# Gated MLP of a small transformer stack: the last product of two hidden groups as seven half products of sums

## The reference

```python
f_in = _rmsnorm(h, g_pre_ffn[l])
gt = jnp.einsum("bsd,df->bsf", f_in, w_gate[l])
up = jnp.einsum("bsd,df->bsf", f_in, w_up[l])
f = jnp.einsum("bsf,fd->bsd", jax.nn.silu(gt) * up, w_down[l])
h = h + _rmsnorm(f, g_post_ffn[l])
```

## Time and profile before

| | |
|---|---|
| runs, median of 3 | 1795.46 us (1795.06 to 1796.2) |
| profiled execution, own time | 1796.07 us |
| its span in the trace | 1794.3 us |
| granted TensorE clock, mean | 0.993 |
| busy: PE, DVE, ACT | 97%, 63%, 45% |

### The profile page before, as it was taken

How to read it: one execution, slowest core, us unless ns; L and a number is a source line. 1 busy time by engine, 2 the same in 40 slices (tenths; PEclk the granted TensorE clock), 3 DMA queues, 4 the chain that set the end, 5 groups by cost and what they waited for, 6 DMA issues and landing times.

```text
span 1794.3 us, 21666 instructions
## 1 busy us (share of the span) xinstructions
PE 1746.8 (97%) x8311; PEld 1435.7 (80%) x8311; DVE 1136.0 (63%) x1988; ACT 808.1 (45%) x1543; POOL 38.1 (2%) x87
## 2 busy tenths in 40 slices
PE   8999999999999999989999999999999999999998
PEld 7887888888887777677888888788887788888886
DVE  6666358787854666865868786488977543243345
ACT  7433344444434656754444344432857532232233
POOL 0000000000001121010000000000000000000000
PEclk9999999999999999999999999999999999999999
DMA  7222443333133111115142312232100333333331
GB/s 248 80 72 85 138 117 94 106 112 89 47 98 83 60 59 60 48 47 176 58 142 71 118 51 90 71 96 92 47 12 14 102 97 106 94 94 98 102 94 59
DMA packets 195751, 158.32 MB, mean 88 GB/s; under 512 B 5248, under 2 KB 161280, under 8 KB 195648
## 3 DMA queue, kind: packets, MB, share of 16 engines
q1 hardware_dynamic: 194240, 154.16, 28.5%
q0 software_dynamic: 400, 1.25, 0.3%
q10 hardware_dynamic: 1008, 1.53, 0.2%
HBM read 154.81 MB, written 2.10 MB: 87 GB/s over the span
## 4 chain that ended last, share of the span: by engine, by line
PE 89%; DVE 6%; ACT 3%; issue 1%; DMA 0%; POOL 0%; DVEq 0%; SPq 0%; ACTq 0%
PE ps L896 29%; PE ps L898 28%; PE ps L897 28%; PE ps L1356 1%; PE ps L952 1%; ACT sb L1827 1%; PE ps L1250 0%; DVE sb L2046 0%; ACT sb L1562 0%; DVE sb L2074 0%; DVE sb L2048 0%; PE ps L1011 0%; DVE sb L2528 0%; PE ps L1221 0%; PE ps L1204 0%
## 5 line engine op out<-in xcount | busy, mean ns | idle before, releaser
L896 PE MATMUL ps<-sb,sb 128*128 128x512 f32 (+4 forms) x2499 | 958.6, 390 | 9.0 <-ACT sb L1827 5.2
L898 PE MATMUL ps<-sb,sb 128*128 128x512 f32 (+4 forms) x2499 | 938.5, 380 | 0.0
L897 PE MATMUL ps<-sb,sb 128*128 128x512 f32 (+4 forms) x2499 | 938.3, 380 | 0.0
L2048 DVE TENSOR_TENSOR sb<-sb,sb 128x512 fp32r<-128x512 f32 x604 | 390.8, 690 | 260.9 <-ACT sb L1562 258.3
L896 PEld LDWEIGHTS ps<-sb,sb 128*128 128x128 f32 (+1 forms) x2499 | 464.0, 188 | 113.9 <-issue 13.6
L1562 ACT ACTIVATE sb<-sb 128x512 fp32r<-128x512 f32 x604 | 347.1, 622 | 440.1 <-PE ps L898 438.2
L898 PEld LDWEIGHTS ps<-sb,sb 128*128 128x128 f32 (+1 forms) x2499 | 463.6, 188 | 89.2
L897 PEld LDWEIGHTS ps<-sb,sb 128*128 128x128 f32 (+1 forms) x2499 | 464.3, 189 | 83.4 <-issue 0.2
L1719 ACT ACTIVATE sb<-sb 128x512 f32<-128x512 f32 x64 | 40.3, 630 | 105.5 <-DVE sb L2321 105.5
L2330 DVE TENSOR_TENSOR sb<-sb,sb 128x1024 fp32r<-128x1024 f32 x42 | 51.4, 1224 | 39.5 <-ACT sb L1724 39.5
L2528 DVE SCALAR_TENSOR_TENSOR sb<-sb,sb,sb 128x512 f32<-128x512 f32 x90 | 67.4, 749 | 1.9
(11 more groups left out here) (216 smaller groups left out, 1082.1 us busy)
## 6 DMA issues: line engine op xcount, KB each, us to landing
sb<-in_w_up SPq DMA_DIRECT2D x86, 512.0 KB, 4.1
sb<-in_w_down SPq DMA_DIRECT2D x86, 512.0 KB, 3.9
sb<-in_w_gate SPq DMA_DIRECT2D x22, 512.0 KB, 3.8
sb<-in_a_w_in SPq DMA_DIRECT2D x20, 512.0 KB, 3.8
sb<-in_w_in SPq DMA_DIRECT2D x20, 512.0 KB, 3.7
sb<-in_w_o SPq DMA_DIRECT2D x16, 512.0 KB, 3.8
sb<-in_w_mem_kv SPq DMA_DIRECT2D x8, 512.0 KB, 7.5
sb<-in_w_out SPq DMA_DIRECT2D x8, 512.0 KB, 3.8
```

The source lines that it names most:

```text
L896: mm(ps, lh, rh, start=start, stop=False, **k)
L897: mm(ps, lh, rl, start=False, stop=False, **k)
L898: return mm(ps, ll, rh, start=False, stop=stop, **k)
L2048: tt(lo, raw, hi, ALU.subtract).then_inc(S("w_lo"), parts)
```

## The change

For the first two groups of the gated MLP the last product is done as seven half products each, as in the squared MLP. The code of `product`, `weight_sum`, `a_sum` and `a_lo` is taken out of the squared MLP to serve both. A second list, `gated_plan`, orders PE, ACT and DVE: half product j of a group is followed by two tiles (one gate, one up) of the next group, in the first group's last place by four, in the second group's last two places by one each. In the groups after the first the gate and up tiles share banks 0 and 1, since 2 to 7 hold half products. Results are added to `F`, now 1024 columns wide, or to `EUG`. The hidden values need both norm factors now, as sums mix tokens: DVE has a new multiplication by `RB` for each hidden tile (`hf`), and `rms2` is gone. The third group is done directly for all columns into eight banks; before it DVE writes `F` (plus `EUG`) into these banks (`pre`), and PE adds on top. So the norm at the end reads both halves from PSUM, and `last_sum` is gone. SP loads quarters of `w_down_2` behind certain slabs. The set of slabs that are split in one piece is named `IN_ONE`, a name that nothing else takes, and has the slabs of the gated MLP as well.

```diff
-    PRODUCTS = [(4, 2, "11", 0), (6, 5, "21", 0), (4, 0, "T2", 2), (6, 1, "11", 1), (2, 6, "12", 3), (6, 3, "22", 0),
-                (2, 4, "21", 4)]
+    ORDER = [[("A11", 4, 2, True, "11", 0), ("A12", 6, 5, True, "21", 0), ("S2", 4, 0, False, "T2", 2),
...
+    ORDER += [[("A11", 4, 3, True, "11", 0), ("S1", 6, 4, True, "11", 1), ("A12", 2, 6, True, "21", 0),
+               ("S2", 4, 0, False, "11", 2), ("S4", 6, 1, False, "22", 0), ("S3", 2, 2, True, "12", 3),
+               ("A22", 2, 5, False, "21", 4)]]
...
+    GATED = [[(2 * j, 2 * j + 1) for j in range(6)] + [(12, 13, 14, 15)],
+             [(2 * j, 2 * j + 1) for j in range(5)] + [(10,), (11,)]]
+    for n in range(16):
+        gated(n)
+    for g in range(2):
+        for j in half_products(2, g):
+            for n in GATED[g][j]:
+                gated(2 * F0[g + 1] + n)
...
-    WIDE = {i for i in QSLAB} | {i for k, i in SL.items() if k[0] == "up" and k[2] > 2}
+    IN_ONE = {i for i in QSLAB} | {i for k, i in SL.items() if k[0] == "up" and k[2] > 2 or k[0] in ("gt", "u2") and k[1] > 1}
...
+            plan += G[0] + [up(n, 0)] + ([("t6", F0[g] + 7)] if g else []) + [
+                ("hf", g, 7), ("S", g, 1), ("h", g, 1), up(n, 1), ws(g, 1, 0), ("rd", g, 0), ("S", g, 2), ("h", g, 2), ws(g, 1, 1)]
+            plan += gate(n, 0)
...
+        for m, b in ((4, "11"), (5, "12"), (6, "21"), (7, "22")):
+            behind[SL["gt", m]] = (2, 0, b)
...
-        for g, f in enumerate(FG):
-            for n in range(2 * f):
-                tile_t(Ah, Al, "pre_ffn", n % 4, lambda: ffn_free(g, n),
...
+                q.wait_ge(S("gate2"), 2 * F0[g] + n - (3 if g == 0 else 1))
+
+        for step in PLAN_G:
+            if step[0] == "G":
+                g, n = step[1:]
+                tile_t(Ah, Al, "pre_ffn", n % (4 if g == 0 else 2), lambda: ffn_free(g, n),
...
+            elif step[0] == "P":
+                product(2, *step[1:])
...
+            if j == 0:
+                q.wait_ge(S("pre"), PRE.index((t, n)) + 1)
...
-                parts = 2 if i in WIDE else 1
+                parts = 2 if i in IN_ONE else 1
...
-            tt(Bl[:, m - F0[g], :], T6[:, m % 2, :], Bh[:, m - F0[g], :].bitcast(F32), ALU.subtract).then_inc(
-                S("h2_lo"), 1)
...
+                tt(HFG[:, m, :], T5[:, m % 2, :], RB[:, :], ALU.mult).then_inc(S("h_sq"), 1)
...
+                    ts(banks[t][:, :], x, 1.0, None, ALU.mult).then_inc(S("pre"), 1)
...
+                    tt(banks[4 * n + t][:, :], x, EUG[:, t % 2, :], ALU.add).then_inc(S("pre"), 1)
...
-        def last_sum(t):
-            q.wait_ge(*strip_done("down2", 0, t))
-            q.wait_ge(S("f_sum"), t + 1)
-            tt(F[:, t, :], banks[t][:, :], F[:, t, :], ALU.add).then_inc(S("f_sum"), 1)
```

More of the change, by code:

```diff
@@ L235, in build @@
         for g in range(3):
[L236 to L240, removed]
+            for j in half_products(l, g):
                 for m in [j] if j < 6 else [6, 7]:
@@ L486, in build @@
+    PLAN_G = gated_plan()
+    PRE = [s[1:] for s in PLAN_G if s[0] == "pre"]
     CV_GROUPS = [range(0, 10), range(10, 20), range(20, 31)]
@@ L1117, in mlp @@
                 elif step[0] == "P":
-                    product(*step[1:])
+                    product(l, *step[1:])
             for n in range(2):
@@ L1436, in mixed_ready, with strip @@
                 q.wait_ge(S("pair_lo"), k - 3)
-        def strip(w, ks, t, b, xh, xl, ready, first, last):
+        def strip(w, ks, t, b, xh, xl, ready, first, last, skip=False):
             _, wh, wl = w
@@ new lines, in out_of_gated @@
+        def out_of_gated(g, j):
+            q.wait_ge(S("w_used"), PS[2, g, j] + 2)
+            x = ORDER[2][j][0]
+            for t in range(2):
+                ps = banks[ORDER[2][j][1] + t][:, :]
+                if x == "S2":
+                    d, before, signal = EUG[:, t, :], out_done(2, g - 1, j, t) if g else None, S("u_sum")
+                else:
+                    t0, n = GOES[x]
+                    d, before, signal = F[:, t0 + t, 512 * n:512 * n + 512], summed.get((t0 + t, n)), S("f_sum")
+                    summed[t0 + t, n] = out_done(2, g, j, t)
+                if before:
+                    q.wait_ge(*before)
+                    tt(d, ps, d, ALU.add).then_inc(signal, 1)
+                else:
+                    ts(d, ps, 1.0, None, ALU.mult).then_inc(signal, 1)
@@ L2739, in vector_program @@
-                weights(SL["u2", m] + 3)
+                q.wait_ge(S("h_sq"), 64 + m - 1)
+                tt(T5[:, m % 2, :], banks[2 * (m - F0[g]) % (4 if g == 0 else 2)][:, :], RB[:, :], ALU.mult).then_inc(
+                    S("gate2"), 1)
+            elif kind == "t6":
+                m = step[1]
+                g = max(g for g in range(3) if F0[g] <= m)
                 q.wait_ge(S("w_used"), SL["u2", m] + 1)
                 q.wait_ge(S("silu"), m + 1)
-                q.wait_ge(S("h2_lo"), m - 1)
```

430 lines of the change are left out of this document (242 added, 188 removed).

## The result

| | before | changed |
|---|---|---|
| median of the runs | 1795.83 us (1795.06 to 1797.32, 4 runs) | 1783.11 us (1782.67 to 1784.04, 4 runs) |
| profiled execution: own time, span | 1796.07, 1794.3 us | 1782.82, 1781.0 us |

The ratio is 0.9929, with a 95% interval from 0.9912 to 0.9946: 12.7 us less, where 12.6 us were forecast; the interval is 3 us wide to either side, so the agreement in the last digit is luck. Timed again later beside the experiments, the changed kernel gave 1783.52 us (5 runs) to 1796.12 us (21 runs) before.

The account below looks back on a forecast made before the run. PE was taken to bound the gated MLP, with DVE and ACT work free there. 1796.07 less 10.88 (matmuls) and 1.74 (end) gave 1783.45 us, or 1782.8 as median, 0.61 lower; range 1781.0 to 1786.0 us.

Parts of the forecast that it names:

- Matmuls: Gated MLP's first two groups: 48 fewer matmuls on PE at a step of 0.2267 us each, saving 10.88 us.
- DVE and ACT hidden: Gated MLP's half products: added DVE and ACT work costs nothing behind PE's packed matmuls, bounds 0 to 3 us.
- the two margins: First group's first half product: slab splits done 1.1 us (gate tile) and 1.2 us (up tile) before PE wants them.
- twice (once a group): If a margin in the first half product were gone, PE would stop zero to perhaps 1 us in each group.
- Loads and splits in one piece: SP's quarter loads, and squared-MLP slabs split whole instead of in halves: both cost nothing, the nearest split deadline leaving 3 us.
- some 55 us: DVE's added busy time: 50 more 1024-wide instructions, 34 more of 512, less 182 slabs at 0.15 us each.
- The end: After PE's last matmul: without `last_sum` PE sets the pace, and the chain falls from 5.35 to 3.61 us, gaining 1.74.
- a condition that the forecast named: Before the third group: `pre` writes for banks wanted first end some 5 us before PE comes, two others some 2 us.
- Rival 2: Gated MLP: a PE wait lowers the clock, costing about 2.5 us more, 9 us for both groups, 1792 us; chance 0.02.
- Rival 3: Gated MLP: DVE overruns its periods, tiles wait for two banks, 1799.6 us; chance 0.03 together with late squared-MLP slabs.

## Why the prediction was right, point by point

**Matmuls: 10.88 us forecast, 10.83 in the trace.** Shown from both ends: the saving between the two matmuls, and 10.84 us in the trace (10.5 by the runs) for 48 matmuls put back. The step of 0.2267 us, taken from first and last start rather than from a row's duration, was the number that mattered.

**DVE and ACT hidden: right, and the two margins were right to 0.1 us** (1.15 us at the first against 1.1). What I added as "twice (once a group)" was wrong: in the second group the sums of weights stand ahead of the half product, so its margins are over 2 us. It changed no number, as nothing was lost in either.

**Loads and splits in one piece: nothing, as forecast.** The forecast of DVE's busy time was "some 55 us" more (its terms add up to 57) and is 59.6, but that is in part luck. It took rows at their durations, 1.22 and 0.69 us, where in a row they are worth their steps, 1.13 and 0.60, and it took 0.15 us for a slab in one piece where its own difference of steps, 0.07, is what the runs show (15 us for 210 slabs); the two errors go against each other. The halves fall from 604 to 208, so 198 slabs changed and not 182. With steps and 198 slabs the sum would be 63.

**The end: 1.74 us forecast, 1.58 in the trace.** The chain was 3.60 us (3.61); the store took some 0.2 us more. The two experiments at the end show DVE's queue as its cause: without the sums the kernel before has 6.65 us there, with two additions more the changed kernel has 7.98. That the end alone brings nothing in the kernel before shows a condition that the forecast named (the writes end before PE comes to their banks) but gave no price for the case that it fails: 1.7 us, as much as the end brings.

**Rival 2's mechanism exists at its price.** A wait of 3.8 us cost 2.7 us more by the clock, where the rival had 2.5. It needed four added instructions to come up there. But not every long wait is paid twice: one of 2.0 us had the lower clock behind it, one of 2.8 us didn't.

**Rival 3's mechanism was wrong.** I had the two banks and DVE's sum of a period as what would break, from a mean of 17.2 us on. No wait for a bank appeared. What breaks first is the way from the gate tile's reading over silu to the next slab's copy, with a margin of 4.6 us in a typical period. The run with six more instructions is slower than the kernel before, though by the forecast's counts its mean period has (14.3 + 4 x 17.8 + 2 x 10.4) / 7 = 15.2 us of DVE work, below the 17.2 that the rival asked for. With the same sum in a better place 20.7 us of it were gone.

## What to carry to other kernels

Where PE's steps are packed, as here, fewer matmuls are worth their start-to-start step each, and work added elsewhere is free up to a margin that belongs to a place, not to a sum. To find it, follow from PE's next deadline backward through every instruction that stands in order on each engine, also those that have nothing to do with the slab (silu ahead of a copy), and test it with instructions that change nothing. A PSUM bank that is filled ahead of an accumulation needs another strip in front of it.

## What was not expected of the hardware

DVE's writes into PSUM, which no row of before had, step like its reads: two in 1.20 us (1743.08 to 1744.28). Ahead of the gated MLP PE's order is the same in both kernels, yet at the same matmul the two executions are up to 2.8 us apart (1266.68 before, 1269.48 after), by where the granted clock is at its lower level, and 0.89 us at the end of it; runs of one kernel are spread over 1 to 5 us.
